# Router logits from the transposed residual, lists and weights as two matmul groups, first two gathers static

## The reference, cut to what matters

```python
x = x + (mix @ w_out)                                   # mixer's output projection, residual
h2 = rms_norm(x, norm2_g).reshape(B * S, -1)            # x / sqrt(mean(x*x) + 1e-6) * norm2_g
p_group = softmax(h2 @ rg_w + rg_b)                     # 4 groups
g_prob, g_idx = lax.top_k(p_group, 1)
e_logits = (h2 @ re_w + re_b).reshape(-1, 4, 4)         # 16 experts, 4 in each group
sel = take_along_axis(e_logits, g_idx)                  # the 4 of the chosen group
top_p, top_i = lax.top_k(softmax(sel), 2)
w = g_prob * top_p / sum(top_p)
for e in range(16):
    y = (silu(h2 @ w_gate[e]) * (h2 @ w_up[e])) @ w_down[e]
    out = out + combine[:, e:e + 1] * y                 # combine holds w at the two chosen experts
return rms_norm(x + out, final_norm_g)
```

## Time and profile before

| | |
|---|---|
| median of 3 runs | 606.22 us (606.18 to 608.25) |
| profiled execution | span 606.8 us (the page gives no other time of it) |
| TensorE busy | 574.4 us (95%) |
| VectorE busy | 421.0 us (69%) |
| ScalarE busy | 349.9 us (58%) |
| GpSimd busy | 135.7 us (22%) |
| DMA | 144.85 MB, mean 239 GB/s |

### The profile page before, as it was taken

The page is one execution under the profiler, slowest core; times in us unless marked ns, Lnnn a source line. Parts: engine busy times, 40 slices in busy tenths (PEclk is TensorE's granted clock), DMA queues, the critical chain, the costliest instruction groups (busy, mean ns, idle before and its releaser), DMA issues.

```text
span 606.8 us, 8244 instructions
## 1 busy us (share of the span) xinstructions
PE 574.4 (95%) x2859; PEld 471.2 (78%) x2860; DVE 421.0 (69%) x559; ACT 349.9 (58%) x457; POOL 135.7 (22%) x116
## 2 busy tenths in 40 slices
PE   4799999999999999997999999999999999999973
PEld 3689878888887888885878888888888888888851
DVE  3811466552683764365399898889989889989857
ACT  4722343585023432350577888878788878788623
POOL 4410000000000000014604442233443233411170
PEclk9999999999999999999899999999999999999997
DMA  8995222022210046796199999999999999993163
GB/s 300 379 372 196 71 69 68 4 69 71 71 45 26 7 167 231 244 397 239 62 311 374 375 372 371 362 374 374 366 389 372 373 372 370 354 384 132 46 251 139
DMA packets 72140, 144.85 MB, mean 239 GB/s; under 512 B 3906, under 2 KB 13290, under 8 KB 71984
## 3 DMA queue, kind: packets, MB, share of 16 engines
q1 hardware_dynamic: 65936, 125.49, 58.5%
q0 software_dynamic: 6176, 19.00, 9.0%
HBM read 132.89 MB, written 14.71 MB: 243 GB/s over the span
## 4 chain that ended last, share of the span: by engine, by line
PE 83%; DVE 7%; DMA 4%; issue 2%; ACT 2%; SPq 1%; POOL 1%; POOLq 0%; DVEq 0%; ACTq 0%
PE ps L1222 23%; PE ps L1224 22%; PE ps L1223 22%; PE ps L1229 5%; DMA arena<-w_in 2%; PE ps L1287 2%; PE ps L1264 2%; PE ps L1237 2%; PE ps L1324 1%; PE ps L1312 1%; DMA arena<-y_dram 1%; PE ps L1278 1%; DVE res L1183 1%; PE ps L1351 1%; DVE act_lo L832 1%
## 5 line engine op out<-in xcount | busy, mean ns | idle before, releaser
L1222 PE MATMUL ps<-hi_ring,act_hi 128*128 128x512 f32 (+1 forms) x608 | 240.9, 396 | 1.2 <-DVE act_lo L832 1.2
L1022 DVE TENSOR_TENSOR lo_ring<-arena,hi_ring 128x2048 fp32r<-128x2048 f32 x94 | 215.1, 2291 | 37.7 <-ACT hi_ring L737 36.6
L1224 PE MATMUL ps<-hi_ring,act_lo 128*128 128x512 f32 (+1 forms) x608 | 233.9, 385 | 0.0
L1223 PE MATMUL ps<-lo_ring,act_hi 128*128 128x512 f32 (+1 forms) x608 | 233.7, 384 | 0.0
L737 ACT ACTIVATE hi_ring<-arena 128x2048 fp32r<-128x2048 f32 x94 | 180.1, 1917 | 20.8 <-PE ps L1224 14.8
L1222 PEld LDWEIGHTS ps<-hi_ring,act_hi 128*128 128x128 f32 x608 | 114.6, 188 | 28.4 <-issue 6.0
L1224 PEld LDWEIGHTS ps<-hi_ring,act_lo 128*128 128x128 f32 x608 | 114.4, 188 | 23.5
L1223 PEld LDWEIGHTS ps<-lo_ring,act_hi 128*128 128x128 f32 x608 | 114.7, 189 | 20.4
L823 DVE TENSOR_TENSOR lo_ring<-arena,hi_ring 128x512 fp32r<-128x512 f32 x68 | 44.9, 686 | 48.3 <-ACT hi_ring L613 47.8
L537 POOL DMA_INDIRECT y_dram<-y,row_info x15 | 16.1, 1072 | 154.8 <-issue 154.8
L832 DVE TENSOR_TENSOR act_lo<-ps,act_hi 128x512 fp32r<-128x512 f32 x64 | 41.5, 682 | 12.3 <-ACT act_hi L775 5.9
(11 more groups left out here) (178 smaller groups left out, 530.5 us busy)
## 6 DMA issues: line engine op xcount, KB each, us to landing
arena<-w_gate SPq DMA_DIRECT2D x32, 1024.0 KB, 12.2
arena<-w_up SPq DMA_DIRECT2D x32, 1024.0 KB, 12.7
arena<-w_down SPq DMA_DIRECT2D x32, 1024.0 KB, 12.5
arena<-w_in SPq DMA_DIRECT2D x16, 512.0 KB, 9.1
y_dram<-arena POOLq DMA_DIRECT2D x8, 512.0 KB, 11.3
arena<-w_out SPq DMA_DIRECT2D x4, 1024.0 KB, 5.1
arena<-y_dram SPq DMA_DIRECT2D x8, 512.0 KB, 7.4
arena<-w_in SPq DMA_DIRECT2D x3, 1024.0 KB, 15.7
```

The lines of the kernel that those rows point to most:

```text
L1022: nc.vector.tensor_tensor(lo(N1 + n12), raw(n12), hi(N1 + n12).bitcast(F32), ALU.subtract).then_inc(lo_done, 1)
L1222: nc.tensor.matmul(dst, a_hi, b_hi, start=start, stop=False)
L1223: nc.tensor.matmul(dst, a_hi, b_lo, start=False, stop=False)
L1224: return nc.tensor.matmul(dst, a_lo, b_hi, start=False, stop=stop)
```

## The change

The logits are no longer taken from h2. The router weights are multiplied by norm2_g once (loaded as a column), the residual itself is turned in halves of 512 columns as soon as a half is there, and its product with the weights is scaled by 1/rms of the token when the bias is added. All 80 columns of logits lie in one bank. The square sums are taken by halves: the first half's mean plus epsilon (Identity) is the bias of the root over the second half. h2 itself is still made and stored, for the gathers.

In the routing, index records, ranks, one-hots and the lists' token and slot come first (`lists_ready`); gate operations, two quarters of slot 1's conversion, the counts, the gate weights and a second group of eight multiplies for the weights come behind it (`weights_made`, `info_made`). GpSimd's first two gathers take all 128 rows with the index straight from `meta`, without a length; the zeroing of the row buffers is gone. Fillers change in number. The first product waits for one half of the rows only.

```diff
-TURN_H2_STEPS = ((N1 - 1, 1), (N1 - 1, 2), (N1 - 2, 3))
-LOGIT_STEPS = ((N1 - 2, 2), (N1 - 2, 3), (N1 - 1, 3))
+TURN_X2_STEPS = ((N1 - 3, 1), (N1 - 3, 2), (N1 - 3, 3), (N1 - 2, 0), (N1 - 2, 1), (N1 - 2, 2), (N1 - 2, 3))
+LOGIT_STEPS = ((N1 - 3, 2), (N1 - 3, 3), (N1 - 2, 0), (N1 - 1, 0), (N1 - 1, 1), (N1 - 1, 2), (N1 - 1, 3))
 # SyncE
-                    sp.wait_ge(lg_ready, T)
+                    sp.wait_ge(lg_ready, 2 * T)
 # GpSimd
+            pool.dma_start(gain2_col, bass.AP(norm2_g.tensor, 0, [[1, P], [P, KD]]), allow_slow_non_contiguous=True
+                           ).then_inc(gain2_col_in, 16)
...
-            pool.wait_ge(h2_turned, 2 * T)
+            pool.wait_ge(lists_ready, 1)
             for b in range(2):
-                nc.gpsimd.memset(x_rows[b], 0.0).then_inc(xg_zero, 1)
-            pool.wait_ge(xg_zero, 2)
-            pool.wait_ge(lists_ready, 1)
+                pool.indirect_dma_start(x_rows[b], None, h2_dram, bass.IndirectOffsetOnAxis(ap=meta[:, 4 * b:4 * b + 1], axis=0),
+                                        bounds_check=last_token, oob_is_err=False).then_inc(rows_in[b], 16)
+            pool.wait_ge(info_made, 1)
...
-            for e in range(2):
-                gather(e, e)
 # ScalarE
+            def copy_x2(half, t):
+                act.wait_ge(x2_turned, T * half + t + 1)
+                if t >= 2:
+                    act.wait_ge(lg_ready, T * half + t - 1)
+                nc.scalar.copy(x2t[t % 2][:, 4 * half:4 * half + 4, :],
+                               ps[:, 4 + t % 2, :].rearrange("p (k s) -> p k s", k=4)).then_inc(x2_copied, 1)
+            def half_square(half, t):
+                act.wait_ge(x2_ready, T * half + t + 1)
...
+                nc.scalar.activation(ps[:, 7, :], res_t[:, t, half * 512:half * 512 + 512], ACT.Square,
+                                     accum_out=total).then_inc(sq_done, 1)
...
+                if half == 0:
+                    nc.scalar.activation(half_mean[:, t:t + 1], total, ACT.Identity, bias=eps[:, 0:1],
+                                         scale=1.0 / D).then_inc(half_done, 1)
+                else:
+                    act.wait_ge(half_done, t + 1)
+                    nc.scalar.activation(rms[:, T + t:T + t + 1], total, ACT.Sqrt, bias=half_mean[:, t:t + 1],
+                                         scale=1.0 / D).then_inc(root_done, 1)
 # VectorE, before the first softmax
+                    dve.wait_ge(rw_in, 32)
+                    dve.wait_ge(gain2_col_in, 16)
+                    nc.vector.tensor_tensor(rw_v, rw_v, gain2_col.unsqueeze(2).to_broadcast([P, KD, N_LOGITS]),
+                                            ALU.mult).then_inc(rw_scaled, 1)
 # VectorE, routing
-            dve.wait_ge(lg_ready, T)
-            step_done(nc.vector.tensor_tensor(lg..., ps[:, 0:T, 0:N_LOGITS], rbias..., ALU.add))
+            norm2(T - 1)
+            dve.wait_ge(lg_ready, 2 * T)
+            for t in range(T):
+                ins = nc.vector.scalar_tensor_tensor(lg[:, t, :, :]..., ps[:, 6, t * N_LOGITS:(t + 1) * N_LOGITS],
+                                                     rms[:, T + t:T + t + 1], rbias[:, :], ALU.mult, ALU.add)
...
+            # two index records; rank lookup; one-hots (each moved up)
+            dve.wait_ge(lists_made, 1)
+            nc.vector.tensor_scalar(meta_v[:, :, 0:2], ps[:, 7, 0:2 * E]..., float(NO_ROW), None, ALU.add).then_inc(lists_ready, 1)
             # gate operations
+            for piece in range(2, 4):
+                split_piece(N1 + 1, piece)
             # counts, gate weights, weight records (weights_set)
             split(2, 2)
+            dve.wait_ge(weights_made, 1)
+            nc.vector.tensor_reduce(meta_v[:, :, 2:3].bitcast(F32), ps[:, 3, 0:2 * E]..., AX_X, ALU.add).then_inc(info_made, 1)
+            rows_lo(0, 1)
             # slots, overflow flags; before, rows_lo(0, 1) stood behind them
             split(3, 3)
 # TensorE
+            def turn_x2(n):
+                half, t = n // T, n % T
+                pe.wait_ge(x2_ready, n + 1)
+                if n >= 2:
+                    pe.wait_ge(x2_copied, n - 1)
+                turn(4 + t % 2, [res_t[:, t, (4 * half + i) * P:(4 * half + i + 1) * P] for i in range(4)]).then_inc(x2_turned, 1)
+            def logits(n):
+                half, t = n // T, n % T
+                if n == 0:
+                    pe.wait_ge(rw_scaled, 1)
+                pe.wait_ge(x2_copied, n + 1)
+                for k in range(4 * half, 4 * half + 4):
+                    ins = nc.tensor.matmul(ps[:, 6, t * N_LOGITS:(t + 1) * N_LOGITS], x2t[t % 2][:, k, :], rw_v[:, k, :], ...)
+                ins.then_inc(lg_ready, 1)
...
-            pe.wait_ge(x2_ready, 2 * T)
-            keep_clock(8, 3)
-            turn_h2(T - 1)
-            keep_clock(4, 3)
-            logits(T - 1)
-            keep_clock(18, 5)
+            keep_clock(4, 0)
+            turn_x2(2 * T - 1)
+            keep_clock(4, 0)
+            logits(2 * T - 1)
+            keep_clock(15, 0)
 # rank multiply
-            keep_clock(16, 5)
-            # eight multiplies for all four fields
+            keep_clock(6, 0)
+            list_fields(7, 0).then_inc(lists_made, 1)
+            keep_clock(14, 0)
+            pe.wait_ge(weights_set, 2)
+            list_fields(3, 2).then_inc(weights_made, 1)
...
-            keep_clock(27, 5)
-            pe.wait_ge(lists_ready, 1)
+            keep_clock(8, 0)
             pe.wait_ge(rows_in[0], 16)
-            pe.wait_ge(h2_copied, 2 * T)
             # turn of the first rows
-            keep_clock(8, 7)
+            keep_clock(4, 0)
+            pe.wait_ge(x_lo, 1)
+            product(0, xt[0], 0, 0, 0, True, False)
             pe.wait_ge(x_lo, 2)
-            product(0, xt[0], 0, 0, 0, True, False)
             product(0, xt[0], 4, 1, 1, False, True)
```

More of the change, by code:

```diff
@@ L674, in mix_hi @@
                                          ACT.Copy).then_inc(m_hi, 1)
[L676 to L683, removed]
+            def copy_x2(half, t):
[6 more added lines that the diff above has]
+                act.wait_ge(x2_ready, T * half + t + 1)
+                if T * half + t:
+                    act.wait_ge(sq_done, T + T * half + t)
+                total = sum_sq[:, T + t:T + t + 1] if half else half_sq[:, t:t + 1]
+                nc.scalar.activation(ps[:, 7, :], res_t[:, t, half * 512:half * 512 + 512], ACT.Square,
+                                     accum_out=total).then_inc(sq_done, 1)
+                act.wait_ge(sq_done, T + T * half + t + 1)
+                if half == 0:
[5 more added lines that the diff above has]
+                                         scale=1.0 / D).then_inc(root_done, 1)
             for g, t in STEPS:
@@ L713, in _ @@
                     mix_hi(1)
[L714 to L720, removed]
+                if g == N1 - 3 and t:
+                    if t >= 2:
+                        copy_x2(0, t - 2)
+                    half_square(0, t - 1)
+                if (g, t) == (N1 - 2, 0):
+                    copy_x2(0, 2)
+                    half_square(0, 3)
+                if (g, t) == (N1 - 1, 0):
+                    copy_x2(0, 3)
+                if g == N1 - 2 and t:
+                    half_square(1, t - 1)
+                if g == N1 - 1 and t:
+                    copy_x2(1, t - 1)
                 if g < N1 - 1:
@@ L1006, in _ @@
                     nc.vector.tensor_tensor(v, v, ps[:, t, :], ALU.add).then_inc(x2_ready, 1)
[L1007 to L1015, removed]
+                if g == N1 - 1 and t < T - 1:
+                    norm2(t)
                 if g < N1 - 1:
                     split_piece(g + 2, t)
+                if (g, t) == (N1 - 2, T - 1):
+                    for piece in range(2):
+                        split_piece(N1 + 1, piece)
             def split(n, n12):
@@ L1043, in _, with rows_lo @@
             g_hot = hot_1[:, :, 0, :]
+            def rows_lo(b, wait):
+                for a in range(2):
+                    row_lo(xt[b][1][:, 4 * a:4 * a + 4, :], 4 + a, xt[b][0][:, 4 * a:4 * a + 4, :], x_hi, wait + a, x_lo)
             def first_max(values, top, eq, cm, hot, fours):
@@ L1138, in _ @@
             nc.vector.tensor_copy(over[:, UNITS + 1:2 * UNITS + 1], flags[cur]).then_inc(over_set, 1)
-            def rows_lo(b, wait):
-                for a in range(2):
-                    row_lo(xt[b][1][:, 4 * a:4 * a + 4, :], 4 + a, xt[b][0][:, 4 * a:4 * a + 4, :], x_hi, wait + a, x_lo)
             def step(b, e, last=False):
@@ L1424, in _ @@
                     turn_mix(1)
-                if (g, t) in TURN_H2_STEPS:
-                    turn_h2(TURN_H2_STEPS.index((g, t)))
+                if (g, t) in TURN_X2_STEPS:
+                    turn_x2(TURN_X2_STEPS.index((g, t)))
                 if (g, t) in LOGIT_STEPS:
@@ L1447, in _, with list_fields @@
             ins.then_inc(rank_ready, 1)
-            keep_clock(16, 5)
-            for c in range(2 * T):
```

(16 more changed lines are left out.)

127 lines of the change are left out of this document (67 added, 60 removed).

## The result

The changed kernel takes 602.55 us (median of 20 runs, 601.30 to 607.39) against 607.08 for the kernel before (20 runs, 604.55 to 608.25) beside it. The ratio is 0.9937, 95% interval 0.9921 to 0.9953. The forecast was 596.6 with a range of 594.0 to 601.5: the direction was right, the size was not. The profiled execution has a span of 602.7 us and a time of 604.35, 1.8 above the median. Of 54 later runs of the kernel before, one took 731.17 us at a granted clock of 0.75; it is left out of every comparison.

A forecast was written before the change was run, and what follows sets the result against it. Bound: a string of small dependent steps, 258.65 to 291.79 us, ahead of a fixed-length expert stage. Between 10.0 us (weights last) and 8.5 (rows last) it took 9.6: 606.2 - 9.6 = 596.6 us, range 594.0 to 601.5.

The forecast's parts named there:

- Logits interleaved: Half turns and half logits among output-projection products: last product ends 2.1 us later, first routing operation 264.7 instead of 266.38.
- Routing: VectorE from first routing operation to the lists: ready at about 272.2 instead of 276.75, 4.55 us won.
- Gather: First gather straight behind the lists, at about 272.5, with all 128 rows; rows land between 277.9 and 281.3.
- Weights: New last wait before the first product: VectorE done at 276.7, first product at 281.8, 10.0 us earlier than 291.79.
- The rule against it: Shared SBUF port: first gather meets two quarter conversions, leaves at about 274.9; up to 0.8 us of the 10.0 lost.
- Moved or delayed, off the path: Later loads, flags and GpSimd slot writes (ending about where they did) cost nothing; third gather has less in hand.
- The sum: Saving of 9.6 us, between 10.0 (weights last) and 8.5 (rows last), taken off the median 606.2: 596.6 us.
- rows come last: Rival: gathered rows are the last wait, first product at 283.3 or later; 597.7 to 599 us; chance 0.22.
- The clock: Rival: TensorE falls to 1.2 GHz in the idle gap before the weights, costing 2 to 4.5 us; chance 0.13.
- The half statistics: Rival: Identity on ScalarE brings table loads, up to 10.2 us, 606.8; chance 0.06 including other stalls.
- The column load: Rival: norm2_g's load of 1024 single elements stalls VectorE before the first softmax; landing after 55 gives 616; chance 0.04.

The follow-up runs named there:

- slots_early: Changed kernel with the five VectorE slot-index operations moved ahead of the first rows' low-part conversion, so slot writes start sooner; 598.88 us, ratio to before 0.9877.
- before_slots_late: Kernel before with GpSimd's eight slot writes moved behind the traffic of experts 12 and 13; 606.36 us, ratio 1.0011.
- before_busy_dve: Kernel before with four unused VectorE subtractions of two SBUF operands (128x1536) added behind the first rows' low part; one run, 607.87 us.

## Where the prediction held and where it failed, by its own steps

| step of the prediction | forecast | measured |
|---|---|---|
| Logits interleaved: last add | 260.8 | 260.99 |
| first routing operation | 264.7 | 264.99 |
| lists ready | 272.2 | 272.4 |
| gather leaves / rows land | 272.5 / 277.9 to 281.3 | 273.27 / 280.53 |
| weight records done | 276.7 | 276.87 |
| first product | 281.8 (weights last) to 283.3 (rows last) | 282.64 |
| slot writes and third gather | about where they were | third gather at 304.05, before 297.04 |

*Logits, Routing, Gather, Weights:* right to within 0.9 us each. The gather left 0.9 us behind the lists, not 0.3, and landed in 7.3 us; so the rows, not the weights, came last by 0.6 us. By the first product this was worth little, as the prediction had said.

*The rule against it:* it was weighed at the wrong place. At the first gather the two quarter conversions cost it 0.25 us (1.27 instead of 1.02). The same meeting at the slot writes cost 6.5 us of GpSimd's time (14.3 against 7.8).

*Moved or delayed, off the path:* this is the step that failed. It said that "GpSimd's slot writes end about where they did". They ended at 301.5 instead of 295.2, and the third gather's rows landed at 313.73. Two views of before held all that was needed. The writes run from 285.25 to 295.20, and the conversions that follow the first product, at 297.00 and 301.48, move with it: 9 to 10 us earlier is 287 and 292, in the middle of the writes. And the gather at 297.04 shows with its 3.13 us what such a meeting costs. I moved TensorE's stage and left the position of VectorE's conversions, which follow it, where it was relative to GpSimd. From the medians of slots_early and of the change, 598.88 and 602.55, this step is worth 3.7 us; with it alone put right, the time lies inside the range. The premise that the end moves one for one with the first product holds once the writes are out of the way: between before_slots_late and slots_early the first product moves by some 7 us (290.19 to 282.81) and the span of the same executions by 6.9 (603.9 to 597.0).

*The sum:* the other 2.3 us (598.88 against 596.6) are a matter of what the saving was taken from. The profiled execution, span 606.8, was one of the long ones: 53 later executions of the kernel before have spans of 602.8 to 607.3, median 605.0, and the time is 1.6 to 3.1 us above the span. The prediction set that span beside the median time of 606.22 as if they were the same measure, and took the whole saving off the median. Spans agree with the sum: 606.8 - 9.6 is 597.2, and the median span of slots_early is 597.2. Part of the saving was a cost that a usual execution does not have in full. In the profiled one the clock was at half until past 292 (granted 0.50 from 290 to 292); in before_busy_dve the first product comes 1.4 us earlier, at 290.44, and in before_slots_late, which has the same order up to there, the chain shows it 1.6 us earlier, straight at full clock:

```profile
287.03 3.15 PE ps L1242 x8
290.19 0.23 PE ps L1227
```

*The rivals:* "rows come last" came in part, by 0.6 us. The clock did fall, but at 314 and not at 284. The half statistics brought no table load: there are 13 in either kernel, and behind 215 us only the Exp load at 263.85 and one at 288.46 ahead of the Silu, 1.28 us each. The column load stalled nothing; VectorE shows no wait for it.

## What to carry to other kernels

When a dense stage is moved forward, move with it in your drawing every engine that it drives, and lay the result over the engines that do not move: here VectorE's conversions slid onto GpSimd's indexed writes. Look in the trace of before for one place where the two already meet, such as one DMA issue that takes 3.13 us among others of 0.97, and use it as the price. The group rows show it too: a mean of 2294 ns for the gathers and of 977 for the slot writes, the same kind of instruction. And take a saving from the execution in which it was measured, or first compare that execution's span with others.

## What the runs showed of the hardware

An indexed DMA that GpSimd issues while VectorE subtracts two SBUF operands (128x1536 or 128x2048) ends 0.82 to 0.89 us behind the subtraction's end. That holds for 173 of the 176 such cases in the ten traces, in which it takes 1.39 to 3.13 us; alone it takes 0.96 to 1.05. A subtraction with one operand in PSUM does not hold it (0.96 and 0.97 in the kernel before). VectorE hardly pays: its subtractions of 128x2048 take 2.28 to 2.37 us with or without. A write that was already running at 287.70 when the subtraction started at 287.71 took its usual 0.97, and the subtraction beside it 2.32. So it is in all 155 cases in which the DMA starts first: it takes 0.93 to 1.01 us, the subtraction at most 2.32. In the other three of the 176 the DMA started less than 0.05 us behind the subtraction and still took 0.97 to 1.01.

The Trainium skill, "SBUF — State Buffer", section "SBUF: two separate sides", states that whichever of the two starts first keeps the shared port for its whole instruction and that the other is blocked for that long. Where VectorE is first, these rows agree. Where GpSimd is first, they do not: the subtraction behind the write at 287.70 was not held for the 0.97 us that the write took, and the measurement decides. The same section reports that a tensor_tensor was not seen to stall a DMA; for indexed DMAs of GpSimd the rows here differ (0.97 us becomes 1.39 to 3.13), and the measurement decides.
